# The modulation matrix of a two-block network: 128 of 144 tiles computed as VectorE row sums instead of TensorE products

## The chip, the cores and the metric

The kernel runs on one core of a Trainium2 chip. The metric is the device time of one launch in microseconds (us), the median of several runs. All data are fp32. Three compute engines matter here: TensorE (PE in the profile) multiplies, ScalarE (ACT) and VectorE (DVE) prepare its operands and take its results away. SyncE (SP) and GpSimd (POOL) only issue DMAs.

## What is computed

A first block of two layers (half-step feed-forward, mixer, half-step feed-forward) on 512 tokens and 256 context tokens of width 1024, then a second block. Each norm, gate and residual of the first block is modulated by columns that depend on the conditioning vectors `c` and `c_ctx` alone:

```python
sc = jax.nn.silu(c)
scc = jax.nn.silu(c_ctx)
for li in range(DEPTH):            # 2 layers
    m = jnp.split((sc @ ada_w[li] + ada_b[li])[:, None, :], N_MOD, axis=-1)    # 9 x 1024
    mc = jnp.split(scc @ ada_w[li] + ada_b[li], N_MOD, axis=-1)
    h = half_ffn(h, norm_g[li, 0], m[0], m[1], m[2], ffn_w_gu[li, 0], ffn_w_down[li, 0])
    hc = half_ffn(hc, norm_g[li, 0], mc[0], mc[1], mc[2], ffn_w_gu[li, 0], ffn_w_down[li, 0])
    ...
    h = half_ffn(h, norm_g[li, 2], m[6], m[7], m[8], ffn_w_gu[li, 1], ffn_w_down[li, 1])
    ...
```

`ada_w` is 2 x 1024 x 9216, 75 MB; it is multiplied with two vectors. In the second layer the context needs only `mc[0]` to `mc[4]`.

## The kernel before

**One stream of weight tiles.** All weights pass through one list, `TILES`, of 559 tiles of up to 128x1024 words: 415 product tiles and 144 modulation tiles (stage `ada`). SyncE loads each into one of four `raw` slots (L324) once the tile four places earlier has been split. ScalarE rounds it to `wh` (L335), VectorE forms the rest `wl = raw - wh` (L342), and TensorE multiplies with both parts: a product tile is 7 or 8 chunks, each chunk three products in two column ranges (L353). The semaphores `w_hi`, `w_lo` and `tile_done` count tiles in the order of the list. Splitting runs `AHEAD` = 2 places ahead of the product.

**Stages.** The feed-forwards are `ffn0` to `ffn3`, each of three parts `up` (16, 14, 14 tiles; gate and value tiles alternate) and `down` (8 tiles; 8, 7, 7 chunks). After `ffn0` stands the even mixer (`ev_in`, `ev_out`), after `ffn2` the odd one. In an `up` stage VectorE takes each even tile away with L677 and L679, ScalarE applies the SiLU (L657), and after each odd tile VectorE runs L677, twice L685, L696 and L698, which make the hidden operand `hidh`, `hidl`. In a `down` stage it adds to the residual (L436); in the third one it also prepares the next norm (L516, L490). The first two tiles of an `up0` stage are multiplied together, chunk by chunk, while the norm's factors are still being made (L541 on TensorE, L551 on ScalarE, the reciprocal L557 on VectorE).

**The modulation before.** 16 `ada` tiles start the program. In `ffn0` and in `ffn1` one `ada` tile stands before every product tile (in `up0` from the third on) until 64 are done. For each, ScalarE and VectorE split it like any other tile, and TensorE does four matmuls (L752) with the four columns `scc` (high and low part of both vectors) as its weights and 512 columns of the tile streaming, into 4 partitions. Four tiles are a block: ScalarE copies its row out (L776), TensorE transposes it back in four small matmuls (L764), VectorE adds the bias (L787 to L797). The transposes stand one tile behind the block's last tile in the order, but for the last block of each of the groups (16, 64, 64): there they follow at once and wait for the copy.

Of the kernel before, what the change touches and what calls it, by code (L numbers as in the profile page):

```python
# [21 lines left out]
ADA_TILES = 144  # L22
ADA_START = 16
ADA_FFN = 64
# [34 lines left out]
class Tile:  # L59

    def __init__(self, n, stage, k):
        self.n, self.stage, self.k = n, stage, k
        self.words = stage.chunks * P if stage.name != "ada" else 2 * 512
        self.slot, self.free = None, None
# [20 lines left out]
def stream(stages):  # L85

    ada = Stage("ada", ADA_TILES, 2, "own_x")
# [17 lines left out]
    assert len(ada.n) == ADA_TILES  # L105
    return tiles, ada


def build(nc, t):
# [5 lines left out]
    TILES, ADA = stream(STAGES)  # L115
    NTILES = len(TILES)
    PROD = [x for x in TILES if x.stage is not ADA]

    ctx = ExitStack()
    with ctx:  # L120
# [66 lines left out]
        adarow = sb("adarow", R_AT + words(16, T), [2, 512])  # L187
        xin = sb("xin", ZH_AT, [6, D])
# [106 lines left out]
        ADA_BEFORE, waiting = {}, []  # L295
        for tile in TILES[ADA_START:]:
            if tile.stage is ADA:
                waiting.append(tile.n)
            else:
                ADA_BEFORE[tile.n], waiting = waiting, []  # L300

        def done(n):
            return n + 1
# [15 lines left out]
        def load_tiles(sp, src):  # L319
            for tile in TILES:  # L320
                n = tile.n
                if n >= NRAW:
                    sp.wait_ge(w_lo, done(n - NRAW))
# [4 lines left out]
        def split_hi(act, n):  # L328
            if n >= NTILES:
                return  # L330
            w = TILES[n].words
            act.wait_ge(raw_loaded[n % NRAW], n // NRAW * 16 + 16)
            if n >= NW:
                act.wait_ge(tile_done, done(n - NW))
            nc.scalar.activation(wh[:, n % NW, 0:w], raw[:, n % NRAW, 0:w], ACT.Copy).then_inc(w_hi, 1)  # L335

        def split_lo(dve, n):
            if n >= NTILES:
                return
            w = TILES[n].words  # L340
            dve.wait_ge(w_hi, n + 1)
            nc.vector.tensor_tensor(wl[:, n % NW, 0:w], raw[:, n % NRAW, 0:w], wh[:, n % NW, 0:w],  # L342
                                    ALU.subtract).then_inc(w_lo, 1)

        def products(pe, stage, xh, xl, ready=None, side=None, then=None, own_ready=None, freed=None):
# [3 lines left out]
            def chunk(n, q):  # L349
                at = TILES[n].slot * 1024  # L350
                for j, (w, x) in enumerate(((wh, xh), (wh, xl), (wl, xh))):
                    for s, e, to in stage.segs:
                        last = nc.tensor.matmul(  # L353
                            psum[:, at + to:at + to + e - s],
                            w[:, n % NW, q * P:(q + 1) * P], x[:, q, s:e],
# [37 lines left out]
        def act_tiles(act, stage, use=None):  # L393
            for k, n in enumerate(stage.n):
                for m in ADA_BEFORE[n]:
                    ada_act(act, m)
# [4 lines left out]
        def dve_tiles(dve, stage, use):  # L401
            for k, n in enumerate(stage.n):
                for m in ADA_BEFORE[n]:
                    ada_dve(dve, m)
# [58 lines left out]
        NPS, NSUM, MT, ADA_ACC = 2048, 3072, 2816, 3072  # L463
# [1858 lines left out]
```

## Time and profile before

| | before |
|---|---|
| median of 3 runs | 3952.47 us (3951.46 to 3954.43) |
| the profiled execution | 3956.19 us |
| its span, first to last instruction | 3954.4 us |
| TensorE busy | 3740.9 us, 95% |
| VectorE busy | 1919.5 us, 49% |
| ScalarE busy | 1116.0 us, 28% |
| mean granted clock of TensorE | 0.963 of full speed |

The span is what the trace covers; 1.8 us lie around it. The trace has windows (busy time by stretch), groups (instructions of one line together) and a timeline (rows in order of time, with the idle time before a row and who ended it in brackets). A clock of 1.00 is 2.4 GHz and 0.50 is 1.2 GHz.

### The profile page before, as it was taken

The page shows a single profiled execution, that of the slowest core. Times are in us where ns is not written, and L with a number is a line of the kernel's source. Part 1 is how long each engine was busy: PE and PEld are TensorE (multiplying, and loading weights), DVE is VectorE, ACT ScalarE, POOL GpSimd, SP SyncE. Part 2 cuts the span into 40 slices and gives each one's busy share as a digit, 9 for nine tenths or more (in the row PEclk, how much of TensorE's full clock was granted, in tenths as well). Part 3 has the DMA queues.
Part 4 walks back from the last instruction along what each step waited for, and adds up shares of the span by engine and source line. Part 5 has one row for each costly group of instructions (what it writes and reads, how often), then busy time and mean ns, then how long its engine had stood idle before and what let it go on. Part 6 is the DMA issues. An engine that isn't in the chain of part 4 may idle for free. (4 is left out here: it accounts for less than half of the span.)

```text
span 3954.4 us, 47312 instructions
## 1 busy us (share of the span) xinstructions
PE 3740.9 (95%) x20148; PEld 3362.6 (85%) x20148; DVE 1919.5 (49%) x2887; ACT 1116.0 (28%) x1602; POOL 15.3 (0%) x32
## 2 busy tenths in 40 slices
PE   7999999988899999999999999999999978888898
PEld 5999999986799999999999999778888777666687
DVE  6534445437654454454333455754336653444434
ACT  5222223134432222231111131443223312222232
POOL 0000000000000000000000000000000000000000
PEclk8999999988999999999999999999999978999999
DMA  5333333200023333331111131012233101111122
GB/s 185 107 118 107 123 107 101 73 22 4 17 69 108 116 108 114 115 97 59 64 62 62 60 103 48 27 49 91 94 98 99 62 1 39 43 45 46 44 83 88
DMA packets 85616, 302.40 MB, mean 76 GB/s; under 512 B 9792, under 2 KB 9984, under 8 KB 85280
## 3 DMA queue, kind: packets, MB, share of 16 engines
q1 hardware_dynamic: 82800, 290.04, 22.5%
q0 software_dynamic: 2608, 9.34, 0.7%
q8 instruction: 160, 2.62, 0.3%
q14 instruction: 48, 0.39, 0.0%
HBM read 297.25 MB, written 2.10 MB: 76 GB/s over the span
## 5 line engine op out<-in xcount | busy, mean ns | idle before, releaser
L353 PE MATMUL psum<-zh,wh 128*128 128x384 f32 (+2 forms) x3792 | 1124.0, 355 | 30.9 <-DVE odnl L1918 7.5
L353 PE MATMUL psum<-zh,wl 128*128 128x384 f32 (+2 forms) x3792 | 1113.9, 352 | 0.0
L353 PE MATMUL psum<-zl,wh 128*128 128x384 f32 (+2 forms) x3792 | 1113.1, 352 | 0.0
L335 ACT ACTIVATE wh<-raw 128x1024 fp32r<-128x1024 f32 (+2 forms) x559 | 564.1, 1026 | 1146.0 <-PE psum L353 1130.9
L342 DVE TENSOR_TENSOR wl<-raw,wh 128x1024 fp32r<-128x1024 f32 (+2 forms) x559 | 658.7, 1191 | 373.9 <-ACT wh L335 372.5
L353 PEld LDWEIGHTS psum<-zh,wh 128*128 128x128 f32 x3792 | 698.5, 190 | 90.2 <-issue 12.2
L353 PEld LDWEIGHTS psum<-zh,wl 128*128 128x128 f32 x3792 | 699.3, 190 | 43.1
L353 PEld LDWEIGHTS psum<-zl,wh 128*128 128x128 f32 x3792 | 700.4, 190 | 40.0
L677 DVE TENSOR_TENSOR scr<-psum,rf 128x768 f32<-128x768 f32 x132 | 126.4, 957 | 490.1 <-PE psum L353 490.1
L353 PE MATMUL psum<-hidh,wh 128*128 128x384 f32 (+1 forms) x1232 | 339.4, 345 | 0.0
L353 PE MATMUL psum<-hidh,wl 128*128 128x384 f32 (+1 forms) x1232 | 338.2, 344 | 0.0
L353 PE MATMUL psum<-hidl,wh 128*128 128x384 f32 (+1 forms) x1232 | 338.2, 344 | 0.0
L436 DVE SCALAR_TENSOR_TENSOR h<-psum,mod,h 128x512 f32<-128x512 f32 x192 | 115.4, 636 | 410.0 <-PE psum L353 410.0
L353 PEld LDWEIGHTS psum<-hidh,wh 128*128 128x128 f32 x1232 | 225.0, 189 | 13.0
L353 PEld LDWEIGHTS psum<-hidh,wl 128*128 128x128 f32 x1232 | 225.2, 189 | 6.9
L353 PEld LDWEIGHTS psum<-hidl,wh 128*128 128x128 f32 x1232 | 225.0, 189 | 6.9
L657 ACT ACTIVATE scr<-scr,gshift 128x512 f32<-128x512 f32 (+1 forms) x132 | 74.1, 608 | 542.3 <-DVE gshift L679 542.3
L752 PE MATMUL psum<-wh,scc 128*4 128x512 f32 x288 | 115.5, 401 | 13.6 <-DVE wl L342 13.6
L752 PE MATMUL psum<-wl,scc 128*4 128x512 f32 x288 | 115.7, 402 | 0.0
L698 DVE TENSOR_TENSOR hidl<-scr,hidh 128x768 fp32r<-128x768 f32 (+1 forms) x88 | 78.5, 892 | 3.1
L417 DVE TENSOR_TENSOR sx<-psum,rf 128x512 f32<-128x512 f32 x36 | 24.9, 692 | 111.6 <-PE psum L353 111.6
L685 DVE SCALAR_TENSOR_TENSOR scr<-scr,psum 128x512 f32<-128x512 f32 (+1 forms) x132 | 76.3, 620 | 2.3
(378 smaller groups left out, 3018.1 us busy)
## 6 DMA issues: line engine op xcount, KB each, us to landing
raw<-in_wup SPq DMA_DIRECT2D x176, 512.0 KB, 3.6
raw<-in_ada_w SPq DMA_DIRECT2D x144, 512.0 KB, 3.5
raw<-in_wdn SPq DMA_DIRECT2D x64, 448.0 KB, 3.5
raw<-in_w_sw SPq DMA_DIRECT2D x36, 512.0 KB, 3.4
raw<-in_wdn SPq DMA_DIRECT2D x32, 512.0 KB, 3.8
raw<-in_od_in SPq DMA_DIRECT2D x16, 512.0 KB, 3.4
raw<-in_w_ga SPq DMA_DIRECT2D x16, 512.0 KB, 3.5
raw<-in_ev_in SPq DMA_DIRECT2D x15, 512.0 KB, 3.5
```

The source lines that it names most:

```text
L335: nc.scalar.activation(wh[:, n % NW, 0:w], raw[:, n % NRAW, 0:w], ACT.Copy).then_inc(w_hi, 1)
L342: nc.vector.tensor_tensor(wl[:, n % NW, 0:w], raw[:, n % NRAW, 0:w], wh[:, n % NW, 0:w], ALU.subtract).then_inc(w_lo, 1)
L353: last = nc.tensor.matmul(psum[:, at + to:at + to + e - s], w[:, n % NW, q * P:(q + 1) * P], x[:, q, s:e], start=(q == 0 and j == 0), stop ...
L417: ins = nc.vector.tensor_tensor(dst[:, k, lead + s:lead + e], acc(n, a, a + e - s), rf[:, to:to + e - s], ALU.mult)
L436: last = nc.vector.scalar_tensor_tensor(h[:, k, s:e], x, col, h[:, k, s:e], ALU.mult, ALU.add)
L657: last = nc.scalar.activation(part, part, ACT.Silu, bias=gshift[:, j // 2 % 2, g:g + 1])
L677: ins = nc.vector.tensor_tensor(to, acc(n, 0, T), rf[:, 0:T], ALU.mult)
L685: ins = nc.vector.scalar_tensor_tensor(p[:, part], p[:, part], acc(n, SHIFT + g, SHIFT + g + 1), gate[:, part], ALU.add, ALU.mult)
L698: nc.vector.tensor_tensor(hidl[:, jj, 0:tok], p, hidh[:, jj, 0:tok], ALU.subtract).then_inc(hid_done, 1)
L752: last = nc.tensor.matmul(psum[0:4, at:at + 512], scc4[:, j % 4 * 2 + c, :], w[:, n % NW, c * 512:(c + 1) * 512], start=(j % 4 == 0 and c ...
```

## The change

128 modulation tiles become a stage `mod`. The host lays the matrix out transposed: a `mod` tile holds 128 outputs as partitions and the 1024 inputs along the row. The vectors `c` and `c_ctx` are loaded as a tile `cb` of 128 partitions x 2 x 1024 (1.05 MB), the same in each partition, and ScalarE applies the SiLU to it (L757 of the new kernel), once at the start and once more in `ev_out`, since the even mixer uses that memory. VectorE multiplies the raw tile with `cb` and sums along the row in one instruction for each vector (L772), one instruction where only `m` is needed (the last 32 tiles): 96 x 2 + 32 = 224. Then a block of four tiles gets its bias as before. TensorE and ScalarE don't see a `mod` tile. `wh` and `wl` slots, `tile_done` and `w_hi` count the other tiles only (`tile.p`); `raw` slots and `w_lo` count all.

The places move as well: 48 tiles in `ffn0`, 40 in `ffn1`, 40 in `ffn2`; one before each tile of a `down` stage and of `up0` from its third tile, one before every second tile of `up1` and `up2`.

```diff
-ADA_TILES = 144
 ADA_START = 16
-ADA_FFN = 64
+MODS = {"ffn0": 48, "ffn1": 40, "ffn2": 40}
...
     for s in stages:
-        if s.name in ("ffn0_up0", "ffn1_up0"):
-            left = ADA_FFN
+        if s.name.endswith("up0"):
+            left = MODS.get(s.name[:4], 0)
         for k in range(s.tiles):
-            if left and not (s.name.endswith("up0") and k < 2):
-                add(ada)
+            if left and (k >= 2 if s.name.endswith("up0") else k % 2 or "_down" in s.name):
+                add(mods)
                 left -= 1
             add(s)
...
         def split_hi(act, n):
-            if n >= NTILES:
+            if n >= NTILES or TILES[n].stage is MODT:
                 return
...
         def split_lo(dve, n):
             if n >= NTILES:
                 return
+            if TILES[n].stage is MODT:
+                mod_rows(dve, n)
+                return
...
             for k in range(first, stage.tiles):
                 n = stage.n[k]
-                for m in ADA_BEFORE[n]:
-                    ada_pe(pe, m)
                 weights(n)
...
         def dve_tiles(dve, stage, use):
             for k, n in enumerate(stage.n):
-                for m in ADA_BEFORE[n]:
-                    ada_dve(dve, m)
+                for m in MODS_BEFORE[n]:
+                    split_lo(dve, m + AHEAD)
                 split_lo(dve, n + AHEAD)
                 use(n, k)
...
+        def c_rows_pool(pool, times):
+            if times:
+                pool.wait_ge(tile_done, done(EO.n[0]))
+                pool.wait_ge(drained, DR[EO.n[0]])
+            pool.dma_start(cb[:], t["c_rows"]).then_inc(cb_in, 16)
+
+        def c_rows_act(act, times):
+            act.wait_ge(cb_in, 16 * times + 16)
+            nc.scalar.activation(cb[:], cb[:], ACT.Silu).then_inc(cb_silu, 1)
+
+        def mod_rows(dve, n):
...
+            dve.wait_ge(raw_loaded[n % NRAW], n // NRAW * 16 + 16)
+            dve.wait_ge(cb_silu, 1 if j < MODS["ffn0"] else 2)
+            dve.wait_ge(w_lo, n)
+            w = raw[:, n % NRAW, :]
+            for g in range(both):
+                last = nc.vector.scalar_tensor_tensor(w if g == both - 1 else psum[:, MOD_AT:MOD_AT + D], w, 1.0,
+                                                      cb[:, g, :], ALU.mult, ALU.mult,
+                                                      accum_out=mod[:, layer, kind, c + i, g:g + 1])
+            last.then_inc(w_lo, 1)
+            if i == 3:
+                dve.wait_ge(w_lo, n + 1)
...
```

VectorE's order in `ffn0_up0`, from the hidden operand of one odd tile to that of the next, before (`wl` is the split, `scr` the value or gate, `gshift` what ScalarE's SiLU waits for):

```order
L698 TENSOR_TENSOR hidl<-scr,hidh 128x768
L342 TENSOR_TENSOR wl<-raw,wh 128x1024 x2
L677 TENSOR_TENSOR scr<-psum,rf 128x768
L679 COPY gshift<-psum 128x2
L342 TENSOR_TENSOR wl<-raw,wh 128x1024 x2
L677 TENSOR_TENSOR scr<-psum,rf 128x768
```

The same place in the changed kernel (lines are those of the new file):

```order
L705 TENSOR_TENSOR hidl<-scr,hidh 128x768
L772 SCALAR_TENSOR_TENSOR psum,mod<-raw,cb 128x1024
L772 SCALAR_TENSOR_TENSOR raw,mod<-raw,cb 128x1024
L351 TENSOR_TENSOR wl<-raw,wh 128x1024
L684 TENSOR_TENSOR scr<-psum,rf 128x768
L686 COPY gshift<-psum 128x2
```

Of two splits between two tiles, the first has become a pair of row sums that stands ahead of the remaining split.

The second place is VectorE at the change from `ffn1_down2` to `ffn2_up0`, before:

```order
L490 TENSOR_TENSOR scr<-scr 128x768
L342 TENSOR_TENSOR wl<-raw,wh 128x1024
L557 RECIPROCAL rf<-rf 128x768
L677 TENSOR_TENSOR scr<-psum,rf 128x768
L679 COPY gshift<-psum 128x2
L342 TENSOR_TENSOR wl<-raw,wh 128x1024
```

and in the changed kernel:

```order
L497 TENSOR_TENSOR scr<-scr 128x768
L772 SCALAR_TENSOR_TENSOR psum,mod<-raw,cb 128x1024
L772 SCALAR_TENSOR_TENSOR raw,mod<-raw,cb 128x1024
L564 RECIPROCAL rf<-rf 128x768
L684 TENSOR_TENSOR scr<-psum,rf 128x768
L686 COPY gshift<-psum 128x2
L351 TENSOR_TENSOR wl<-raw,wh 128x1024
```

The split before the reciprocal was that of the stage's third product tile; a `mod` tile has its place now, and the third tile's split is the one behind `gshift`, which before was the fourth's.

## Rows read from the trace of the kernel before

**Rows 1.** The page's busy times: engine, busy us, share of the span, instructions
```profile
PE 3740.9 (95%) x20148; PEld 3362.6 (85%) x20148; DVE 1919.5 (49%) x2887; ACT 1116.0 (28%) x1602; POOL 15.3 (0%) x32
```

**Rows 2.** TensorE by windows: length, busy us, clock, DMA share, GB/s
```profile
90.00:480.00 390.00, 390.00 (x2180) 1.00 0.34 112
...
1800.00:2200.00 400.00, 400.00 (x2279) 1.00 0.19 63
```

**Rows 3.** Groups of ScalarE's splits and of the transposes: busy us, mean ns, idle before
```profile
L335 ACT ACTIVATE wh<-raw 128x1024 fp32r<-128x1024 f32 (+2 forms) x559 | 564.1, 1026 | 1146.0 <-PE psum L353 1130.9 <-DMA raw<-in_ada_w 9.8 <-PE psum L752 5.2
...
L764 PE MATMUL psum<-ident,adarow 4*128 4x4 f32 x144 | 15.1, 207 | 10.4 <-ACT adarow L776 10.4
```

**Rows 4.** VectorE's timeline in ffn0_up0: start, length, row, idle before
```profile
96.78 0.96 DVE L677 TENSOR_TENSOR scr<-psum,rf 128x768 f32<-128x768 f32 x1 [3.87 <-PE psum L353]
...
100.43 2.36 DVE L342 TENSOR_TENSOR wl<-raw,wh 128x1024 fp32r<-128x1024 f32 x2
106.17 0.96 DVE L677 TENSOR_TENSOR scr<-psum,rf 128x768 f32<-128x768 f32 x1 [3.38 <-PE psum L353]
...
124.98 0.96 DVE L677 TENSOR_TENSOR scr<-psum,rf 128x768 f32<-128x768 f32 x1 [3.40 <-PE psum L353]
...
134.92 0.96 DVE L677 TENSOR_TENSOR scr<-psum,rf 128x768 f32<-128x768 f32 x1 [4.42 <-PE psum L353]
```

**Rows 5.** The same in ffn2_up0, which has no modulation tiles before
```profile
1806.17 0.96 DVE L677 TENSOR_TENSOR scr<-psum,rf 128x768 f32<-128x768 f32 x1 [4.09 <-PE psum L353]
...
1814.65 0.96 DVE L677 TENSOR_TENSOR scr<-psum,rf 128x768 f32<-128x768 f32 x1 [3.61 <-PE psum L353]
```

**Rows 6.** TensorE's timeline: the last transposes of ffn0 and of ffn1
```profile
666.28 0.58 PE L764 MATMUL psum<-ident,adarow 4*128 4x4 f32 x4 [3.61 <-ACT adarow L776]
...
1745.97 0.41 PE L764 MATMUL psum<-ident,adarow 4*128 4x4 f32 x4 [3.61 <-ACT adarow L776]
```

**Rows 7.** VectorE's timeline in ffn0_down2 and ffn1_down2, residual rows
```profile
661.78 1.14 DVE L436 SCALAR_TENSOR_TENSOR h<-psum,mod,h 128x512 f32<-128x512 f32 x2 [1.71 <-PE psum L353]
...
676.66 1.14 DVE L436 SCALAR_TENSOR_TENSOR h<-psum,mod,h 128x512 f32<-128x512 f32 x2 [8.41 <-PE psum L353]
...
683.94 1.14 DVE L436 SCALAR_TENSOR_TENSOR h<-psum,mod,h 128x512 f32<-128x512 f32 x2 [2.04 <-PE psum L353]
...
1741.47 1.14 DVE L436 SCALAR_TENSOR_TENSOR h<-psum,mod,h 128x512 f32<-128x512 f32 x2 [1.50 <-PE psum L353]
...
1755.46 1.14 DVE L436 SCALAR_TENSOR_TENSOR h<-psum,mod,h 128x512 f32<-128x512 f32 x2 [7.43 <-PE psum L353]
```

**Rows 8.** TensorE by windows behind two of its waits, columns as in Rows 2
```profile
77.00:81.00 4.00, 3.93 (x14) 0.61 0.40 131
...
666.00:670.00 4.00, 3.72 (x14) 0.50 0.51 142
```

**Rows 9.** Timelines: TensorE's third product tile in ffn0_up0, ffn1_up0; VectorE taking the first away
```profile
77.07 0.62 PE L353 MATMUL psum<-zh,wh 128*128 128x384 f32 x2 [3.12 <-DVE wl L342]
...
87.38 0.96 DVE L677 TENSOR_TENSOR scr<-psum,rf 128x768 f32<-128x768 f32 x1 [4.45 <-PE psum L353]
...
1157.01 1.01 PE L353 MATMUL psum<-zh,wh 128*128 128x384 f32 x2 [2.56 <-DVE wl L342]
```

**Rows 10.** Timelines at the start of ffn2_up0: TensorE's third product tile, VectorE's next split
```profile
1788.95 0.59 PE L353 MATMUL psum<-zh,wh 128*128 128x384 f32 x2 [0.22 <-DVE gshift L679]
...
1790.94 1.23 DVE L342 TENSOR_TENSOR wl<-raw,wh 128x1024 fp32r<-128x1024 f32 x1 [2.14 <-ACT wh L335]
```

**Rows 11.** Groups of VectorE by shape: busy us, mean ns, idle before
```profile
L490 DVE TENSOR_TENSOR scr<-scr 128x768 f32<-128x768 f32 x35 | 33.2, 950 | 0.1
L516 DVE SCALAR_TENSOR_TENSOR zl<-h,amul,zh 128x512 fp32r<-128x512 f32 x40 | 29.7, 744 | 0.8 <-ACT zh L506 0.8
...
L516 DVE SCALAR_TENSOR_TENSOR zl<-h,amul,zh 128x256 fp32r<-128x256 f32 x40 | 19.1, 477 | 0.0
...
L1198 DVE TENSOR_TENSOR rsum<-rsum,esink 128x1 f32<-128x1 f32 x48 | 7.2, 149 | 0.0
```

**Rows 12.** All engines by windows, 10 to 15 us: busy us of PE, PEld, DVE, ACT, POOL, then clock, DMA share, GB/s
```profile
10.00:15.00 5.00, 5.00 (x25) 3.17 (x22) 1.84 (x2) 2.12 (x2) 0.00 (x0) 1.00 1.02 402
```

More of the change, by code:

```diff
@@ L85, in stream @@
 def stream(stages):
-    ada = Stage("ada", ADA_TILES, 2, "own_x")
+    ada, mods = Stage("ada", ADA_START, 2, "own_x"), Stage("mod", sum(MODS.values()), KD, "own_x")
     tiles, left = [], 0
@@ L97, in stream @@
     for s in stages:
-        if s.name in ("ffn0_up0", "ffn1_up0"):
-            left = ADA_FFN
+        if s.name.endswith("up0"):
+            left = MODS.get(s.name[:4], 0)
         for k in range(s.tiles):
-            if left and not (s.name.endswith("up0") and k < 2):
-                add(ada)
+            if left and (k >= 2 if s.name.endswith("up0") else k % 2 or "_down" in s.name):
+                add(mods)
                 left -= 1
             add(s)
-    assert len(ada.n) == ADA_TILES
-    return tiles, ada
+    for p, tile in enumerate(x for x in tiles if x.stage is not mods):
+        tile.p = p
+    assert len(mods.n) == mods.tiles
+    return tiles, ada, mods
 def build(nc, t):
@@ L114, in build @@
     ST = {s.name: s for s in STAGES}
-    TILES, ADA = stream(STAGES)
+    TILES, ADA, MODT = stream(STAGES)
     NTILES = len(TILES)
-    PROD = [x for x in TILES if x.stage is not ADA]
+    PROD = [x for x in TILES if x.stage is not ADA and x.stage is not MODT]
     ctx = ExitStack()
@@ new lines, in mod_finish @@
+        def mod_finish(dve, layer, kind, c, both, ins):
+            m = mod[:, layer, kind, c, 0:both]
+            if kind % 3 == 1:
+                link(dve, "dve", ins)
+                ins = nc.vector.scalar_tensor_tensor(amul[:, layer, kind // 3, c, 0:both], m, 1.0,
+                                                     bc(ngain[:, layer, kind // 3, c], [P, 4, both]),
+                                                     ALU.add, ALU.mult)
+            elif kind in (2, 8):
+                link(dve, "dve", ins)
+                ins = nc.vector.tensor_scalar(m, m, 0.5, None, ALU.mult)
+            ins.then_inc(mod_done, 1)
@@ L2252, in lay_out @@
     aw = f["ada_w"].reshape(2, 4, 2, P, 18, 512).transpose(0, 4, 1, 3, 2, 5).reshape(2, 18, 4, P, 1024)
-    first = [0, 2, 1, 3] + list(range(4, 18))
-    a["ada_w"] = np.ascontiguousarray(np.concatenate([aw[0][first], aw[1]]).reshape(ADA_TILES, P, 1024))
+    first = [0, 2, 1, 3]
+    a["ada_w"] = np.ascontiguousarray(aw[0][first].reshape(ADA_START, P, 1024))
+    rows = f["ada_w"].transpose(0, 2, 1).reshape(2 * NMOD * KD, P, D)
+    a["mod_w"] = np.ascontiguousarray(rows[ADA_START:])
+    a["c_rows"] = np.ascontiguousarray(np.broadcast_to(np.stack([f["c"][0], f["c_ctx"]]), (P, 2, D)))
     a["adab"] = np.ascontiguousarray(f["ada_b"].reshape(2, NMOD * KD, P).transpose(2, 0, 1))
```

72 lines of the change are left out of this document (39 added, 33 removed).

## The prediction

> **What bounds the kernel now.** I read the busy times first: TensorE is busy for 95% of the span, VectorE for 49%, ScalarE for 28% [rows 1]. Shares are means, so I read the two stretches that matter by windows: from 90 to 480 us, in `ffn0` with modulation tiles, TensorE is busy for 390.00 of 390 us at a clock of 1.00, and from 1800 to 2200 us, in `ffn2` without them, for 400.00 of 400 us, also at 1.00 [rows 2]. In these stages the end is set by TensorE's own list of instructions. Whatever leaves that list shortens the run, as long as what stays is fed in time. DMA is at a third there, so 40 more loads in `ffn2` find room.
>
> **What leaves TensorE.** (a) *The matmuls.* The first VectorE row after each product tile waits for TensorE, so the distance of two such rows is the period of a tile. With a modulation tile between them it is 106.17 - 96.78 = 9.39 us [rows 4], without one 1814.65 - 1806.17 = 8.48 us [rows 5]. A modulation tile costs 0.92 us. 128 tiles leave the list. Two of them save nothing: the first of `ffn0` and of `ffn1` ran just before a wait of 3.12 and 2.56 us for the split of the third product tile [rows 9]; without it the wait starts earlier and ends at the same time. 126 x 0.92 = 115.9 us.
>
> (b) *The transposes.* Every fourth period is longer: 134.92 - 124.98 = 9.94 against 9.40 us, so 0.53 us for a block's four transposes and what stands between [rows 4]. Of the 144 transposes, 36 blocks [rows 3], the first four blocks stay, and the last one of each feed-forward is counted next: 30 x 0.53 = 16 us.
>
> (c) *The two group ends.* There the transposes follow their tile at once, and TensorE waits 3.61 us for ScalarE's copy, both times [rows 6]. The clock is then 0.50 of full, that is 1.2 GHz, for some us [rows 8]. The whole is seen in the residual rows: 676.66 - 661.78 = 14.88 us where a tile of 683.94 - 676.66 = 7.28 and a modulation tile of 0.92 would take 8.20, so 6.7 us; in `ffn1` 1755.46 - 1741.47 = 13.99, so 5.8 us [rows 7]. Both go, with nothing late behind them: 12.5 us.
>
> Together 115.9 + 16 + 12.5 = 144.4 us.
>
> **What is added.** (d) *The row sums on VectorE.* The trace has no sum along the row with this instruction. The nearest row is the same instruction with two sources in SBUF: 744 ns for 512 columns, 477 for 256 [rows 11], so 267 ns for each 256 more and 744 + 2 x 267 = 1.28 us for 1024. For the accumulated column I add one tiny instruction, 0.15 us [rows 11]. I take 1.4 us a sum, 2.8 us for a tile with two. The lower bound is 1.19 us, the same row less the overlap with its neighbour (about 0.09 us, as the two splits of 1.22 us take 2.36 [rows 4]). An upper bound, double the row, is a rival below. By the Trainium skill, "VectorE: DVE Perf Modes", section "Two Vector instructions with no wait between them", an operation with accumulator output is two instructions; no row here shows its price.
>
> Is it hidden? The tightest place in `up0` is behind an odd tile. TensorE ends it at 96.78; VectorE makes the hidden operand until 100.43, 3.65 us later [rows 4]; then come 2.8 us of row sums and 1.14 of the split for the tile that TensorE wants 8.48 us after 96.78. 3.65 + 2.8 + 1.14 = 7.6 us, and 8.0 where a block's bias follows. It fits by 0.5 to 0.9 us. In `up1` and `up2` the row sums stand every second tile, behind the cheap even one; in `down` the residual takes 1.14 us [rows 7], and in the third one about 3.1 with the norm's 0.74 + 0.48 and 0.95 [rows 11], less overlaps. The one place that does not fit is the second tile of `down1` and `down2`: 7.6 against a period of 7.28 [rows 7]. That is 0.3 us at four places with two sums (in `ffn2` the tiles there have one): 1 us; between 0 and 3.
>
> (e) *`ffn2_up0`.* Its third product tile was split before the norm's reciprocal and started at 1788.95 after a wait of 0.22 us. Now its split is the one that follows `gshift` and ScalarE's SiLU; before, the split in that place began at 1790.94 and took 1.23 [rows 10]. TensorE starts at 1792.2, 3.2 us later, as in `ffn0` and `ffn1` already. Such a wait also costs clock: it is 0.61 in the window behind the one of `ffn0` [rows 8], and that tile took 87.38 - 77.07 = 10.31 instead of 8.48 us [rows 9], 1.8 us; behind the 3.61 us of `ffn0_down2` it was 676.66 - 666.28 - 0.4 (transposes) - 7.28 = 2.7 [rows 6, 7]. I take 2.2: 5.4 us. (f) In `ffn0` and `ffn1` the wait there grows by 0.92 to about 4.0 and 3.5 us, and I add 0.5 us of slow clock each: 1 us.
>
> (g) *The start.* `cb` is 1.05 MB on top of a stretch in which the DMA share is 1.02 at 402 GB/s and ScalarE waits for the loads [rows 12]: 1.05 MB / 402 GB/s = 2.6 us; 0 if the loads behind it have slack. (h) The SiLU of `cb` at the start takes the place of the split of the first modulation tile on ScalarE, which then waits for the norm's sums anyway; the one in `ev_out` stands between two tiles for which ScalarE has one split and one square each. ScalarE at 28% [rows 1] loses 128 splits of 1.03 us [rows 3]. I cost both at nothing; uncovered, one over 2048 columns would be twice a split, 2.1 us. POOL's wait for the first tile of `ev_out` holds up only loads for the odd mixer, a feed-forward and more later.
>
> Costs: 1 + 5.4 + 1 + 2.6 = 10 us. Net 144.4 - 10 = 134.4 us. The profiled execution would take 3956.2 - 134.4 = 3821.8; it stands 3.7 us above the median, so I forecast 3952.5 - 134.4 = **3818 us**. Its own range: clock losses and start at their low ends and no late split give 3811, clock losses of 4 us, 3 us of late splits and an uncovered SiLU give 3830.
>
> **Rivals.** *Half-rate sums.* If a row sum takes twice the row, about 2.5 us, a tile with two takes 5 us. Behind an odd tile of `up0`: 3.65 + 5 + 1.14 = 9.8 against 8.48, 1.3 us late at 7 + 7 + 4 places (of `ffn2`'s tiles eight there have two sums); the second tile of `down0` 1.4 late twice, of `down1` and `down2` 2.5 late four times; `ffn0_down2` 3.1 + 5 + 1.1 = 9.2 against 7.3, three times 1.9. Sum 23 + 3 + 10 + 6 = 42 us, less the 1 counted: 3859 us, and up to 3905 if each of the 27 waits costs 1.7 us of clock as well. For it: nothing in the trace sums along a row this way. Against it: the instruction without the sum runs at full rate [rows 11]. This is what the Trainium skill says outright, in "Vector Engine (DVE) Microarchitecture Reference", section "7. Points that are easy to get wrong": this instruction with two fp32 sources in SBUF halves its throughput, no port being left for the accumulator. The trace disagrees for the form without a sum, and is silent on the one with it.
>
> *Slower than before.* The same place, a higher price: from 3.7 us a sum (three times the row) the late splits eat the gain. At 3.7 us behind an odd and an even tile of `up0` VectorE needs 1.1 + 3.65 + 2 x (7.4 + 1.14) = 22 us for 17 us of TensorE, 5 us late 18 times = 90, and in `down0` and `down1` 1.14 + 7.4 + 1.1 = 9.6 against 8.3 (7.28 x 8/7) and 7.3, 16 x 1.3 + 16 x 2.3 = 58: 148 against 144. 3966 us and up. Nothing speaks for a third of the rate but that both outputs, one into PSUM and one over its own source, are new.
>
> *Contention.* VectorE is nearly always busy in `up0` and reads one more tile from SBUF; should TensorE's matmuls stretch by 2% over the some 160 product tiles among row sums (8 us each, 1300 us), 26 us are lost: 3844 us. Nothing in the rows excludes it; against it, TensorE's clock and busy share are the same in `ffn0`, where VectorE has one split more for each tile, as in `ffn2` [rows 2].
>
> **How the numbers follow.** Forecast 0.79, half-rate 0.13, contention 0.05, slower 0.03. The range goes from the forecast's low end, a little below, to where the half-rate case begins: 3808 to 3856. A measurement of this kernel can tell 0.2%, 8 us, from no change; all cases but one are far on the fast side: faster 0.96, same 0.01, slower 0.03.
>
> **What would show it.** In the new profile: 16 tiles' worth of the small matmuls, 64 in each group; 16 transposes; L677's period in `ffn0_up0` at 8.48 throughout; no 3.61 us wait for `adarow` after 60 us; a wait of 3 to 4 us for the split at the third tile of all three `up0` stages with a slow clock behind it; row sums of 1.2 to 1.4 us; the first product tile some 2.6 us later. It is wrong if TensorE shows waits for `wl` behind odd tiles (the sum is slow), if the period is above 8.48 with TensorE fully busy (contention), or if the clock in the stages is below 1.00.

## The result

| | before | after |
|---|---|---|
| median of 4 runs | 3951.97 us (3951.41 to 3954.43) | 3821.95 us (3818.18 to 3822.56) |
| the profiled execution | 3956.19 us | 3818.18 us |
| mean granted clock of TensorE | 0.963 | 0.962 |

The ratio is 0.9668, 95% interval 0.9651 to 0.9685: 130 us less, where 134.4 were forecast. The same pair measured again (e1_again) gave 133.8 us less, 0.9659 (0.9646 to 0.9672). The forecast of 3818 us lies 4 us below the first median and 1 us below the second. The executions of the unedited kernel before fall into two groups, 3951 to 3957 us at a mean clock of 0.962 or 0.963 and 3964 to 3968 us at 0.958 or 0.959 (6 of the 23 measured beside e9 to e11, all 7 beside e5 to e8); why is open, and so e5 to e8 are compared by their product tiles.

The page of the kernel after (engine, busy us, share of the span, instructions; compare [rows 1]):

```profile
span 3816.4 us, 46071 instructions
PE 3601.0 (94%) x19508; PEld 3305.8 (87%) x19508; DVE 2024.9 (53%) x3175; ACT 979.4 (26%) x1445; POOL 16.4 (0%) x34
```

TensorE has 640 instructions fewer, which is 128 tiles x 4 matmuls and 128 transposes. It is busy for 139.9 us less, about what the span lost: it was the bound and still is. VectorE took on 105 us and ScalarE gave up 137, and neither is near its limit.

TensorE by windows (length, busy us, clock, DMA share, GB/s; compare [rows 2]):

```profile
90.00:480.00 390.00, 390.00 (x2223) 1.00 0.35 114
...
1800.00:2200.00 400.00, 399.39 (x2293) 1.00 0.29 93
```

It is full in the stages with row sums too, and its clock is 1.00. The DMA share of `ffn2` rose from 0.19 to 0.29 and TensorE shows nothing of it (`ffn2` ends at 2193 us here, so the last 7 us of the second window are the next stage's).

VectorE's timeline in `ffn0_up0` (start, length, row, idle time before it and who ended it; compare [rows 4]):

```profile
100.86 0.96 DVE L684 TENSOR_TENSOR scr<-psum,rf 128x768 f32<-128x768 f32 x1 [4.03 <-PE psum L362]
...
104.52 1.23 DVE L772 SCALAR_TENSOR_TENSOR psum<-raw,cb 128x1024 f32<-128x1024 f32 x1
105.66 0.14 DVE L772 DVE_READ_ACCUMULATOR psum<-raw,cb 128x1 f32 x1
105.66 1.22 DVE L772 SCALAR_TENSOR_TENSOR raw<-raw,cb 128x1024 f32<-128x1024 f32 x1
106.81 0.08 DVE L772 DVE_READ_ACCUMULATOR raw<-raw,cb 128x1 f32 x1
106.93 0.17 DVE L779 TENSOR_TENSOR mod<-mod,adab 128x8 f32<-128x8 f32 x1
107.13 0.17 DVE L791 TENSOR_SCALAR mod<-mod 128x8 f32<-128x8 f32 x1
107.21 1.22 DVE L351 TENSOR_TENSOR wl<-raw,wh 128x1024 fp32r<-128x1024 f32 x1
109.34 0.96 DVE L684 TENSOR_TENSOR scr<-psum,rf 128x768 f32<-128x768 f32 x1 [0.92 <-PE psum L362]
...
117.82 0.96 DVE L684 TENSOR_TENSOR scr<-psum,rf 128x768 f32<-128x768 f32 x1 [4.03 <-PE psum L362]
```

The period is 109.34 - 100.86 = 8.48 us and 117.82 - 109.34 = 8.48 us, that of `ffn2` before [rows 5]. A row sum takes 1.23 us, and the next instruction starts 1.14 us after its start, beside the read of the accumulator. The tile with two sums, two bias rows and the split (104.52 to 108.43) is done 0.92 us before VectorE is needed again.

**Where the 138 us between the two profiled executions lie.** The semaphore `tile_done` counts product tiles in the trace, so the time from one tile to another can be compared across kernels:

| us | before | after | difference |
|---|---|---|---|
| start to the first product tile | 72.0 | 74.8 | +2.8 |
| `ffn0` | 619.2 | 548.5 | -70.7 |
| even mixer to the first tile of `ev_out` | 251.4 | 249.6 | -1.8 |
| `ffn1` | 617.5 | 547.0 | -70.5 |
| `ffn2` | 558.5 | 563.3 | +4.8 |
| odd mixer to the first tile of `od_out` | 294.7 | 292.1 | -2.6 |

All other stretches agree within 0.3 us. The stages that the change touches give -133.6 us, the forecast was -134.4. The two mixers, which it doesn't touch, give the other -4.4. That isn't the scatter of single executions: the second trace of each kernel repeats it (before 251.4 and 251.7 in the even one, 294.7 and 294.8 in the odd one; after 249.6 and 249.2, 292.1 and 292.0). But it doesn't come with the row sums either: kernels that differ from these two in a tile's place or a wait take 249.2 to 254.1 us in the even mixer and 292.0 to 296.5 in the odd one. What sets it is open.

TensorE's timeline at the third product tile of `ffn0_up0`, `ffn1_up0` and `ffn2_up0` (compare [rows 9, 10]):

```profile
81.19 1.01 PE L362 MATMUL psum<-zh,wh 128*128 128x384 f32 x2 [5.38 <-DVE wl L351]
...
1087.31 1.01 PE L362 MATMUL psum<-zh,wh 128*128 128x384 f32 x2 [3.48 <-DVE wl L351]
...
1651.95 0.62 PE L362 MATMUL psum<-zh,wh 128*128 128x384 f32 x2 [3.48 <-DVE wl L351]
```

These are the only waits for a split. The one of `ffn0` was forecast at 4.0 us and is 5.38, which the prediction had not foreseen.

### The profile page after: what moved, and what is told of

It reads as the page before. It is cut to its first block, busy times and chain, and to the rows that moved or that the text cites. A ratio compares the mean times of both kernels' runs of the same rounds, so it can differ in the third digit from the quotient of the medians.

```text
span 3816.4 us, 46071 instructions
## 1 busy us (share of the span) xinstructions
PE 3601.0 (94%) x19508; PEld 3305.8 (87%) x19508; DVE 2024.9 (53%) x3175; ACT 979.4 (26%) x1445; POOL 16.4 (0%) x34
## 4 chain that ended last, share of the span: by engine, by line
PE 87%; DVE 9%; ACT 2%; issue 2%; DMA 1%; SPq 0%; DVEq 0%; ACTq 0%
PE psum L362 74%; PE psum L1166 2%; PE psum L989 2%; PE psum L1174 2%; PE psum L1183 2%; DVE nmx L1230 1%; PE psum L1002 1%; PE psum L1642 1%; DVE ev_s L1227 1%; DMA raw<-in_ada_w 0%; PE psum L1651 0%; DVE wl L351 0%; PE psum L1655 0%; ACT wh L341 0%; DVE sw_s L1227 0%
## 5 line engine op out<-in xcount | busy, mean ns | idle before, releaser
L362 PEld LDWEIGHTS psum<-zh,wh 128*128 128x128 f32 x3792 | 700.4, 190 | 84.4 <-DVE wl L351 17.3
L351 DVE TENSOR_TENSOR wl<-raw,wh 128x1024 fp32r<-128x1024 f32 (+2 forms) x431 | 509.4, 1182 | 322.7 <-ACT wh L341 322.1
L341 ACT ACTIVATE wh<-raw 128x1024 fp32r<-128x1024 f32 (+2 forms) x431 | 434.4, 1020 | 839.2 <-PE psum L362 619.6
L772 DVE SCALAR_TENSOR_TENSOR raw<-raw,cb 128x1024 f32<-128x1024 f32 x128 | 156.2, 1220 | 1.4
L772 DVE SCALAR_TENSOR_TENSOR psum<-raw,cb 128x1024 f32<-128x1024 f32 x96 | 117.8, 1227 | 3.7 <-DVE wl L351 0.5
```

What stands on the lines that cost most here:

```text
L341: nc.scalar.activation(wh[:, wslot(n), 0:w], raw[:, n % NRAW, 0:w], ACT.Copy).then_inc(w_hi, 1)
L351: nc.vector.tensor_tensor(wl[:, wslot(n), 0:w], raw[:, n % NRAW, 0:w], wh[:, wslot(n), 0:w], ALU.subtract).then_inc(w_lo, 1)
L362: last = nc.tensor.matmul(psum[:, at + to:at + to + e - s], w[:, wslot(n), q * P:(q + 1) * P], x[:, q, s:e], start=(q == 0 and j == 0), st ...
L772: last = nc.vector.scalar_tensor_tensor(w if g == both - 1 else psum[:, MOD_AT:MOD_AT + D], w, 1.0, cb[:, g, :], ALU.mult, ALU.mult, accum ...
```

## The experiments

My theory after the result: the gain is the sum of the parts that left TensorE (144 us), less three waits at third tiles and a later start; the row sums are hidden. Rivals: the sums cost something everywhere and the matmuls were worth more; or the group ends or the third tiles have another size. The times below are medians with their range and, as a ratio to the kernel before measured beside them, the 95% interval.

**e1_again.** The kernel after, unchanged.

> The changed kernel once more, unchanged, beside the three edits of it below, so that they stand against a run of the same chip. Its median before was 3821.95 us, but the profiled execution took 3818.18 and that of the kernel before 3956.19, against 3951.97 in the median: 138.0 us between the profiled ones, 130.0 between the medians. By product tiles the two traces differ by 133.6 us up to the third tile of ffn2_up0 if the 1.8 us of the even mixer are left out, where nothing was changed. Theory: the change is worth 130 to 134 us, and the rest is spread of single executions in the mixers, up to 4 us. Then this profile shows the stages ffn0 to ffn2 as in the first one within 1 us and another sum in the mixers; median 3820 to 3823. Rival: the change itself moves the mixers by -4 us; then this profile shows the same -1.8 and -2.6 us there as the first.

3819.27 us (3814.31 to 3821.62), ratio 0.9659 (0.9646 to 0.9672). By product tiles it repeats after in `ffn0` (548.6) and `ffn2` (563.3 us). `ffn1` takes 545.7 us, 1.3 less, all of it at the third tile: the wait is 3.48 us again, and the tile behind it is 1.3 us shorter. The mixers show -2.2 and -2.7 us against before, where after had -1.8 and -2.6; that was the rival's sign.

**e9_before.** The kernel before, unchanged.

> The kernel before, unchanged, for a second profile of it. In the first three jobs its median was 3951.97, 3953.1 and 3965.05 us, while the other kernels of the last job agree with the jobs before to 2 us by their product tiles. Theory: the stages ffn0 to ffn2 repeat to 0.5 us, and what differs between its executions lies in the mixers and the second block, which no edit touches. Then this profile has the same tile times up to ev_out as the first one, and ev_out 0 either at 1072.8 (then the 1.8 to 2.2 us in the changed kernels' mixers come with the change) or near 1071 (then they are spread). Rival: the modulation tiles' stages vary themselves; then differences appear inside ffn0 or ffn1.

3954.26 us (3951.24 to 3967.93), ratio 0.9996 (0.998 to 1.0012); by tiles it repeats before within 1 us up to `ffn2` (start 72.8, `ffn0` 618.3, `ffn1` 617.5, `ffn2` 558.4). The 0.9 us of `ffn0` is one step, that of the group end: 13.99 us instead of 14.88, behind the same wait of 3.61 us, so a little of the expectation's rival came as well. The first tile of `ev_out` ends at 1073.1 us, the sign that the expectation had named for a difference between the kernels' mixers and not between executions.

### What the sums cost when they are hidden, and when they are not

**e8_double_sums.** Each row sum is done twice.

```diff
             for g in range(both):
+                link(dve, "dve", nc.vector.scalar_tensor_tensor(psum[:, MOD_AT:MOD_AT + D], w, 1.0, cb[:, g, :],
+                                                                ALU.mult, ALU.mult, accum_out=junk[:, g:g + 1]))
                 last = nc.vector.scalar_tensor_tensor(w if g == both - 1 else psum[:, MOD_AT:MOD_AT + D], w, 1.0,
...
+                if g < both - 1:
+                    link(dve, "dve", last)
```

> The changed kernel with every row sum done twice (the additional one's result goes to a spare column, and three waits on VectorE's own writes are added), so that a tile with two sums costs about 4.9 us on VectorE instead of 2.29: the price of the half-rate rival. Theory: the sums are free only as long as VectorE ends behind an odd tile within 8.48 us. 3.65 + 4.9 + 1.14 = 9.7 us is 1.2 late at 18 places (22 us), 1.4 twice in down0, 2.4 at the four second tiles of down1 and down2, about 1.7 three times in ffn0_down2: 39 us in all, 3860 us, and up to 3905 if each of the 27 waits costs 1.7 us of slow clock. Rival: VectorE has more room than this count gives, and the time stays within 10 us of the changed kernel's 3820.

3877.03 us (3875.25 to 3878.3). By product tiles it is slower than after by 27.0 us in `ffn0`, 18.6 in `ffn1` and 8.1 in `ffn2`. Its timeline in `ffn0_up0`, first VectorE, then TensorE; its waits from 90 to 640 us (sum, count, longest); and its windows:

```profile
105.19 1.23 DVE L773 SCALAR_TENSOR_TENSOR psum<-raw,cb 128x1024 f32<-128x1024 f32 x1
...
110.70 1.22 DVE L352 TENSOR_TENSOR wl<-raw,wh 128x1024 fp32r<-128x1024 f32 x1
```

```profile
111.97 0.62 PE L363 MATMUL psum<-zh,wh 128*128 128x384 f32 x2 [2.00 <-DVE wl L352]
```

```profile
PE psum L363 <- DVE wl L352: 20.0, 10, 2.6
```

```profile
90.00:620.00 530.00, 509.89 (x2866) 0.99 0.33 106
...
112.00:122.00 10.00, 10.00 (x57) 1.00 0.55 182
```

With 5.5 us of sums and bias before the split (105.19 to 110.70) TensorE waits 2.00 us. In the kernel after this part takes 2.7 us and the slack can be read as 0.92 us of idle VectorE; 2.8 us more than that should be late by 1.9, and it is 2.0. So the sums are hidden, by about 0.9 us at this place, and the 224 additional sums cost 54 us. The four sums take 5.2 us here (105.19 to 110.42; about 0.5 of it are the three added waits), near the 5 us of the half-rate rival, so this run tells that rival from the forecast.

The 3877 us are 18 above the 3859 that I had worked out for the rival (3860 in the expectation of this run, whose own rival of 3820 is out). That sum was wrong in count and in price. I had 27 late tiles; the trace has 21 waits of 1.6 to 2.6 us for a split beside those of the third tiles (and one of 0.2): 15 in `up0` instead of 18, and 6 in `down` stages instead of 9. 17 of these tiles take 1.9 to 2.8 us longer than in after, at a clock of 1.00. The other four take 3.8 to 4.4 us longer, 1.5 or 1.6 more than their like, with a slow clock behind the wait; I had put 1.7 us behind each for the 3905. One of the four is the same place in `ffn1_up0` as the one above in `ffn0_up0`, with the same wait:

```profile
1144.39 0.62 PE L363 MATMUL psum<-zh,wh 128*128 128x384 f32 x2 [2.00 <-DVE wl L352]
```

```profile
1146.00:1150.00 4.00, 4.00 (x17) 0.64 0.36 122
```

### What a modulation tile and a group end are worth

**e5_one_matmul.** The kernel before with one of the four matmuls of each of the 128 tiles.

```diff
                 for i, w in enumerate((wh, wl)):
+                    if j >= ADA_START and (c or i):
+                        continue
...
```

> The kernel before, with one of four matmuls left for each of the 128 modulation tiles in ffn0 and ffn1 (the product of the high part of the first 512 inputs' half stays; the other three are left out, so the modulation values are not the reference's). Loads, splits, transposes and waits all stay. Theory: TensorE's list sets the time, so each matmul is worth its 0.23 us: 128 x 3 x 0.23 = 88 us less, 86.5 without the two tiles ahead of the third product tile's wait: 3866 us. Rival: part of the 130 us came from freed ScalarE and VectorE time (128 splits less on each) and not from TensorE's list; then this kernel gains clearly less than 86 us, because the splits are still there.

3878.08 us (3871.06 to 3883.92), ratio 0.9779 (0.9764 to 0.9793). By product tiles `ffn0` takes 577.0 and `ffn1` 576.5 us, 42.2 and 41.0 less than before: 83.2 us for three quarters of the matmuls. VectorE's period:

```profile
96.14 0.96 DVE L677 TENSOR_TENSOR scr<-psum,rf 128x768 f32<-128x768 f32 x1 [3.20 <-PE psum L353]
...
104.86 0.96 DVE L677 TENSOR_TENSOR scr<-psum,rf 128x768 f32<-128x768 f32 x1 [2.71 <-PE psum L353]
```

8.72 us against 9.39 with four matmuls [rows 4] and 8.48 with none [rows 5]: 0.24 us for the one left, 0.67 for the three taken. 126 x 0.67 = 84.4 us; the 83.2 hold a third tile of `ffn1` that took 1.5 us longer than in before, behind a wait. The split of the tile by ScalarE and VectorE is still there and costs nothing. The median is 12 us above the expected 3866, but it is 87.0 us below that of the kernel before measured beside it (3965.05), where 86.5 were expected. The second block of this kernel is some 10 us longer in its trace than in the others (part of it from the end of `ffn3` to the first attention, 308.8 against 301.8 us). Its mean clock is 0.957, where the others have 0.960 to 0.963; the cause stays open.

**e6_ends_late.** The kernel before with the transposes of each group's last block moved behind the next product tile.

```diff
                 last.then_inc(tile_done, 1)
+                while ends:
+                    ada_turn(pe, ends.pop(), late=True)
...
+            if b is not None and j + 1 in ADA_ENDS[1:] and not late:
+                ends.append(n)
+                return
```

> The kernel before, with the transposes of the last block of ffn0 and of ffn1 moved behind the next product tile, so that ScalarE's copy has a whole tile's time. Theory: the two waits of 3.61 us and the slow clock behind them were worth 6.7 + 5.8 us, of which about 0.5 us each stays for the transposes: 11.5 us less, 3941 us, and a tile period of 7.3 to 7.8 us there in place of 14. Rival: the copy's lateness comes from something that moves with it, and the wait appears at the new place: then the gain is under 6 us. It also tells whether the even mixer, 1.8 to 2.2 us shorter in the changed kernel's traces, is so in another kernel whose mixer is the same.

3941.92 us (3940.64 to 3947.42), ratio 0.9943 (0.9928 to 0.9958). By product tiles the step at the group end falls from 14.88 and 13.99 to 8.23 us in both, so 6.65 + 5.76 = 12.4 us, where term (c) had 12.5; the four transposes come back as 0.53 us in the step behind, each time, so the edit is worth 11.3 us, where 11.5 were expected (the expected period of 7.3 to 7.8 had left out the modulation tile's 0.92). The 23 us between this median and that of the kernel before beside it can't be put to the edit, since the latter is some 12 us above that kernel's other medians. TensorE's timeline there, and the window that answers to [rows 8]:

```profile
668.93 0.41 PE L778 MATMUL psum<-ident,adarow 4*128 4x4 f32 x4
669.27 0.61 PE L353 MATMUL psum<-hidh,wh 128*128 128x384 f32 x2
```

```profile
666.00:670.00 4.00, 4.00 (x26) 1.00 0.43 131
```

No wait, and the clock is 1.00 where it had been 0.50. All work is still done, so both the 3.61 us and the slow tile behind them belong to the wait [rows 6]. By e9_before, where the step of `ffn0` was 13.99 too, the same two ends come to 11.5 us: the slow part varies.

### The three third tiles

**e2_third_first.** In `up0` the first row sums stand before the fourth product tile, not the third, so that the third is split before the norm's reciprocal.

```diff
-            if left and (k >= 2 if s.name.endswith("up0") else k % 2 or "_down" in s.name):
+            if left and (k >= 3 if s.name.endswith("up0") else k % 2 or "_down" in s.name):
```

> The changed kernel with its first row-sum tile of each up0 stage one place later, behind the third product tile instead of ahead of it, so that the third tile is split two places ahead again, before the norm's reciprocal, and not behind gshift and the SiLU. Theory: the 5.38 us and the two 3.4 us waits at the third tile, with the slow clock behind each, come from this order alone. In the changed kernel the third tile ends 16.53, 15.01 and 13.76 us after the second; in ffn2 of the kernel before, which had this order, 8.92. So 7.6 + 6.1 + 4.8 = 18.5 us less: 3803 to 3804 us. Rival: the wait only moves to the fourth tile, whose split then stands behind a pair of row sums and the hidden operand: 1.1 + 2.3 + 3.65 + 1.14 = 8.2 us after the second tile, against 8.9 wanted, which just fits; if it does not, half or more of the 18.5 us stays.

3804.06 us (3799.72 to 3804.87), ratio 0.962 (0.9607 to 0.9633). From the second product tile to the third:

| us | before | after | e1_again | e2 | e4 | e8 |
|---|---|---|---|---|---|---|
| `ffn0_up0` | 14.32 | 16.53 | 16.57 | 9.48 | 14.31 | 16.72 |
| `ffn1_up0` | 13.51 | 15.01 | 13.74 | 8.93 | 15.01 | 13.54 |
| `ffn2_up0` | 8.92 | 13.76 | 13.74 | 8.93 | 13.77 | 13.69 |

Together 18.0 us less than after, at three tiles, and 9.4 less than before (whose steps in `ffn0` and `ffn1` hold a modulation tile of 0.92 us each): these waits are older than the change, which had lengthened two and added one. No other step of the three feed-forwards becomes longer, so the wait doesn't move to the fourth tile. The medians show 15.2 us against e1_again; the odd mixer takes 2.7 us more in this trace. TensorE and VectorE of e2 in `ffn0_up0`:

```profile
75.41 0.59 PE L362 MATMUL psum<-zh,wh 128*128 128x384 f32 x2 [0.78 <-DVE gshift L686]
```

```profile
66.33 1.23 DVE L351 TENSOR_TENSOR wl<-raw,wh 128x1024 fp32r<-128x1024 f32 x1 [0.26 <-ACT wh L341]
...
69.25 4.95 DVE L564 RECIPROCAL rf<-rf 128x768 f32<-128x768 f32 x1 [1.70 <-ACT rf L558]
```

The split stands ahead of the reciprocal, in time in which VectorE waited anyway, and TensorE starts at 75.41 instead of 81.19.

**e7_two_ffns.** The 128 tiles stand in `ffn0` and `ffn1` alone, 64 each, before every tile from the third on.

```diff
-MODS = {"ffn0": 48, "ffn1": 40, "ffn2": 40}
+MODS = {"ffn0": 64, "ffn1": 64}
...
-            if left and (k >= 2 if s.name.endswith("up0") else k % 2 or "_down" in s.name):
+            if left and (k >= 2 or not s.name.endswith("up0")):
```

> The changed kernel with the row sums placed as the modulation tiles were before: 64 in ffn0 and 64 in ffn1, one before every product tile from the third of up0 on, none in ffn2. Theory: VectorE hides a pair of sums behind every tile (a tile with two took 2.29 us; behind an odd tile the next split ends 0.9 to 1.3 us early in up0, and up1 and up2 become the same), and ffn2's third tile is again split early: 4.8 us less than the changed kernel, 3815 to 3817 us. The tightest place is ffn0_down2, where the split ends 0.8 us early. Rival: sums behind every odd tile of up1 and up2 come too late where a block's bias and a stage's end meet; then waits for the split cost more than the 4.8 us, and it is at or above 3820.

3818.01 us (3815.83 to 3820.48), ratio 0.9628 (0.9614 to 0.9642). By product tiles `ffn0` takes 548.8, `ffn1` 546.8 and `ffn2` 558.5 us: 4.8 less than after, at `ffn2`'s third tile, and 0.3 us or less elsewhere. So the +4.8 us of `ffn2` is this one place, and VectorE could carry the denser sums of `up1` and `up2` as well. The median is 1 us above the expected 3815 to 3817 and only 1.3 below e1_again, and can't show the 4.8; the odd mixer takes 296.5 us in this trace.

**e4_swap_wait.** ScalarE waits for the constants before it waits for `cb`.

```diff
-            c_rows_act(act, 0)
             wait_consts(act)
+            c_rows_act(act, 0)
```

> The changed kernel with ScalarE's wait for the constants put ahead of the SiLU of cb instead of behind it. In the changed kernel that wait and the wait for the norm's sums follow each other with no instruction between them, and the table load for the square root stands at 69.54 us, behind the wait for the sums; before, it stood at 62.03, ahead of it. Theory: two waits in a row put the table load behind the second, which lengthens the norm's chain by 1.28 us, and that is why the third tile of ffn0_up0 waits 5.38 us and not 4.0. Then the load stands at about 66.4 us here, the wait is 4.1 us, and the median falls by 1.3 to 2 us. Rival: the SiLU before it decides the place; then nothing changes.

3816.7 us (3816.2 to 3819.08), ratio 0.9655 (0.9642 to 0.9668); the median, 2.6 us below e1_again, can't tell this from after. The trace can: the step at `ffn0`'s third tile is 2.2 us shorter (the table above) and no other step moves. ScalarE before the first factors of the norm, in before, after and e4:

```profile
62.03 1.28 ACT L551 ACT_TABLE_LOAD   x1
...
66.71 0.90 ACT L551 ACTIVATE rf<-psum,eps_c 128x768 f32<-128x768 f32 x1 [3.40 <-PE psum L541]
```

```profile
64.45 1.90 ACT L757 ACTIVATE cb<-cb 128x2048 f32<-128x2048 f32 x1
69.54 1.28 ACT L558 ACT_TABLE_LOAD   x1 [3.19 <-PE psum L548]
70.83 0.90 ACT L558 ACTIVATE rf<-psum,eps_c 128x768 f32<-128x768 f32 x1
```

```profile
63.65 1.90 ACT L757 ACTIVATE cb<-cb 128x2048 f32<-128x2048 f32 x1
65.57 1.28 ACT L558 ACT_TABLE_LOAD   x1
69.47 0.90 ACT L558 ACTIVATE rf<-psum,eps_c 128x768 f32<-128x768 f32 x1 [2.62 <-PE psum L548]
```

Before, the load of the function table ran while ScalarE had nothing to do, and the wait for TensorE's sums came behind it. In after it is the other way round: the wait, then 1.28 us of table load on the path to the reciprocal. In e4, where an instruction (the SiLU of `cb`) stands between the two waits, the load is ahead of the wait again. TensorE of e4:

```profile
79.83 0.62 PE L362 MATMUL psum<-zh,wh 128*128 128x384 f32 x2 [4.04 <-DVE wl L351]
```

4.04 us is what the prediction had for after. The rule that two waits without an instruction between them put the load behind the second fits all 13 traces: in after, e1_again, e3, e7 and e8 the two waits follow each other and the load stands behind; in the other eight an instruction stands between them (in before the split of the first modulation tile, in e2, e10 and e11 that of the third product tile) and the load is ahead. Only e4 was made to show it, and I haven't seen how the place is chosen. The 7.0 us of e2 at `ffn0`'s third tile hold this part too.

### The start

**e3_late_rows.** The load of `cb` waits until the last piece of `x` has landed.

```diff
         def c_rows_pool(pool, times):
+            if not times:
+                pool.wait_ge(x_in[5], 16)
```

> The changed kernel with the first load of cb (1.05 MB) issued only when the last tile of x has landed, after about 20 us instead of at 6. Theory: the first product tile of the changed kernel ends 2.79 us later than before because these bytes stand among loads that fill the DMA engines (2.6 us forecast). Then the first product tile ends at about 72 us as before instead of 74.77, and the median falls by 2.5 to 3 us to about 3819. Rival: the delay comes from elsewhere in the start (no later load changes it): tile at 74.8, median as e1.

3816.77 us (3814.85 to 3819.83), ratio 0.9655 (0.9642 to 0.9669). The first product tile is done at 71.5 us, against 74.8 in after, 74.2 in e1_again and 72.0 in before. POOL's issue of the load, and ScalarE's waits for modulation tiles in the first 60 us (sum, count, longest), first in after, then in e3:

```profile
6.14 0.54 POOL L753 DMA_DIRECT2D cb<-in_c_rows  x1
...
ACT wh L341 <- DMA raw<-in_ada_w: 13.4, 7, 3.4
```

```profile
22.66 0.54 POOL L755 DMA_DIRECT2D cb<-in_c_rows  x1 [16.52 <-DMA xin<-in_xin]
...
ACT wh L341 <- DMA raw<-in_ada_w: 10.0, 7, 2.4
```

16.5 us later, the same 1.05 MB delay the first tile no more; ScalarE waits 3.4 us less for its loads. Over all traces the first product tile is done at 73.6 to 75.2 us in the six kernels with the early load and at 71.2 to 72.8 in the seven others. As in e4, the median moves by less than its range (2.5 us against e1_again).

### The pieces together

**e10_first_late** is e2 and e3 together, **e11_two_first_late** the places of e7 from the fourth tile on (the diff is against e7), with e3:

```diff
-            if left and (k >= 2 or not s.name.endswith("up0")):
+            if left and (k >= 3 or not s.name.endswith("up0")):
```

> The changed kernel with both gains of e2 and e3: the third product tile split ahead of the first row sums in all three up0 stages, and the load of cb after the last tile of x. Theory: they are independent, so e2's 18 us and about 2.8 us add up: 21 us less than the changed kernel, 3798 to 3801 us, the first product tile at 72 us. Rival: with the third tile ready early, the start is bound by the norm's chain and the later load buys nothing: 3804 us as e2.

> As e10, but with the row sums of e7: 64 each in ffn0 and ffn1, one before every product tile, none in ffn2. Theory: once the third tile is split early, ffn2 loses nothing by its row sums, so the place of the 128 tiles no longer matters as long as VectorE hides them: within 1 us of e10. Rival: the tighter places in ffn0_down2 and ffn1_down2, where sums, norm and split leave 0.8 us, show waits of 0.5 us and more: 3 us above e10 or worse.

3800.85 us (3800.6 to 3802.32), ratio 0.961 (0.9595 to 0.9625), and 3799.16 us (3798.35 to 3802.85), ratio 0.9607 (0.9591 to 0.9622). They are the fastest versions, 21 to 23 us below after and 18 to 20 below e1_again, and can't be told apart. The two have the same stages by product tiles: `ffn0` 541.5 and 541.5, `ffn1` 540.9 and 540.8, `ffn2` 558.5 and 558.4 us. The page of e10 and TensorE's waits from 55 to 640 us (sum, count, longest):

```profile
span 3799.2 us, 46070 instructions
PE 3597.7 (95%) x19508; PEld 3302.7 (87%) x19508; DVE 2024.6 (53%) x3175; ACT 979.3 (26%) x1445; POOL 16.3 (0%) x34
```

```profile
PE psum L362 <- DVE ev L429: 1.0, 1, 1.0
PE psum L362 <- DVE gshift L686: 0.8, 1, 0.8
PE psum L362 <- DVE h L443: 0.3, 1, 0.3
```

2.1 us of waits are left in 585. `ffn2` has 40 row-sum tiles in e10 and none in e11 (nor in before), and takes 558.5 us with them and 558.4 without.

## Why the prediction was right

**The bound.** TensorE's own list was the bound, and what left it shortened the run. e10 lets the terms be read without the waits: its `ffn0` and `ffn1` are 77.7 and 76.6 us shorter than before, of which 4.82 (14.32 to 9.50) and 4.58 (13.51 to 8.93) at the third tiles. The rest, 72.9 + 72.0 = 144.9 us, is (a) + (b) + (c), forecast at 144.4.

**(a), (b), (c).** (a) and (c) were measured apart: 0.92 us a tile holds (period 8.48 throughout, e5's 8.72 between), and the two ends are 12.4 us (e6) against 12.5. No run was made for (b), but the steps of before and e10, compared tile by tile, show it: 94 steps are shorter by 0.93 us on average, 30 by 1.44, and the two group ends by 7.6 and 6.7. So a block's transposes are worth 0.52 us, and (b) is 15.5 us against 16; (a) is 126 x 0.93 = 117 against 115.9.

**(d) The sums, mis-sized upwards.** I had 1.4 us a sum, 2.8 a tile. The groups of the line, shortest, median and longest in ns:

```profile
L772 DVE SCALAR_TENSOR_TENSOR raw<-raw,cb x128: 1211/1220/1226, 68.1 to 2046.0; 128x1024 f32<-128x1024 f32 x128
L772 DVE DVE_READ_ACCUMULATOR raw<-raw,cb x128: 76/82/84, 69.3 to 2047.2; 128x1 f32 x128
L772 DVE SCALAR_TENSOR_TENSOR psum<-raw,cb x96: 1220/1225/1234, 67.0 to 1708.3; 128x1024 f32<-128x1024 f32 x96
L772 DVE DVE_READ_ACCUMULATOR psum<-raw,cb x96: 134/141/144, 68.1 to 1709.5; 128x1 f32 x96
```

Start to start a sum takes 1.14 to 1.15 us. The extra instruction that I had added at 0.15 us is there, as the Trainium skill says in "VectorE: DVE Perf Modes", section "Two Vector instructions with no wait between them" (an operation with accumulator output is two instructions), but it runs beside the next one and costs nothing. With 2.3 us a tile the second tile of `down1` fits, and the 1 us of late splits never came. There are also three such places with two sums, not the four of the prediction (`ffn1_down2` has no `mod` tile); these three tiles take 7.36 to 7.38 us instead of 7.28. VectorE there, in `ffn0_down1`:

```profile
393.87 1.09 DVE L351 TENSOR_TENSOR wl<-raw,wh 128x896 fp32r<-128x896 f32 x1
395.24 1.14 DVE L443 SCALAR_TENSOR_TENSOR h<-psum,mod,h 128x512 f32<-128x512 f32 x2 [0.29 <-PE psum L362]
```

0.29 us of idle time behind the split: it fits narrowly. At 1.4 us a sum it would not have.

**(e), (f) The third tiles.** Forecast +5.4 for `ffn2` and +1 for `ffn0` and `ffn1` together, 6.4 us; the steps say +4.84, +2.21 and +1.50, 8.6 us. In `ffn2` the wait was as forecast (3.48 less 0.22, where I had 3.2) and the clock cost 1.6 instead of 2.2. In `ffn1` the wait was 3.48 as forecast, and its growth by 0.92 us cost 1.5 of clock in this trace, not 0.5; in e1_again, the same kernel, it cost 0.2, and the three steps come to 7.3 us instead of 8.6. In `ffn0` the wait grew by 2.26: 0.92 as forecast, and 1.3 for the table load (with 0.9 of clock behind them), which is the cover that (h) lost. I had written that the SiLU of `cb` costs nothing since ScalarE waits for the norm's sums anyway. The SiLU itself did cost nothing; what I didn't ask is what else had been hidden in that wait.

**(g) The start.** Forecast 2.6, measured 2.8 (2.6 between the means of the six and the seven traces named under e3), and e3 takes it back.

So 1 + 6.4 + 2.6 = 10 us of costs were 0 + 8.6 + 2.8 = 11.4, and 144.4 us of gain were 144.9. By the terms this is 133.5 us, and by the stages 133.6. That it lies within 1 us of the 134.4 is partly luck: the third tiles were put 2.2 us too low, and the late splits (1 us too high) and the gain (0.5 too low) made up for most of it. The 4.4 us of the two mixers stand in no term.

**The rivals.** *Half rate*: the sum with fp32 sources both in SBUF takes 1.22 us for 1024 columns, where the rows of before for 512 and 256 columns, carried on to 1024, give 1.28 for the form without a sum. The rule of the Trainium skill, "Vector Engine (DVE) Microarchitecture Reference", section "7. Points that are easy to get wrong", does not hold here, and the measurement decides. *Slower* falls by the same row. *Contention*: the period is 8.48 us and the window of 390 us is full at a clock of 1.00; 2% would have been 0.17 us a tile. `ffn2` with 40 row-sum tiles and without any differs by 0.1 us in 558 (e10 and e11), so less than 0.01 us a tile.

## What to carry to other kernels

Price a change on a full engine by the period between two rows that wait for it, with and without the thing removed; then ask of each place where the order is rearranged which split (or load, or table) was hidden in a wait and now stands behind it. A short operation put ahead of a preparation that used to run in a gap costs more than its own time: here one place in the list, the third tile of each `up0`, was worth 18 us in the traces, against 134 for the whole change. And an added load belongs after those that the first computation waits for.

## What the runs showed of the hardware

- **What a wait of TensorE costs in clock isn't set by its length.** Of 21 waits of 1.6 to 2.6 us (e8), 17 were followed by a clock of 1.00, and four were followed by a clock of 0.64 to 0.82 and a tile 1.5 or 1.6 us longer. The tile behind a wait of 3.48 us took 1098.85 - 1087.31 - 8.48 = 3.1 us longer in `ffn1` and 1.8 in `ffn2`; in e1_again, the same kernel, it took 1.8 in `ffn1` too. The one behind 5.38 us took 2.7 longer. The window of the kernel after behind the 5.38 us:

```profile
81.00:85.00 4.00, 3.81 (x12) 0.50 0.42 131
```

- **A sum along the row adds no time that shows** to a VectorE multiply of two fp32 tiles (1.22 us for 128x1024; 1.28 by the shorter rows without a sum), with an output into PSUM or over its own source, and the read of the accumulator (0.14 or 0.08 us) runs beside the next instruction.
- **A table load can move behind a wait** and onto the path through what stands between two waits: 1.28 us of load, 2.2 us at the tile that waits (e4).
